# Matmuls of constants on TensorE in three pauses of a two-layer transformer kernel

## The chip, the core and the metric

The kernel runs on one core of one Trainium2 chip. A core has five engines with instruction queues of their own, which are synchronised by semaphores: TensorE (PE in the profile; its loads of stationary operands are listed apart, as PEld) for matmuls and transposes, VectorE (DVE), ScalarE (ACT), GpSimd (POOL), and SyncE (SP), which here only starts DMAs. TensorE reads SBUF and writes PSUM, which has eight banks; DVE and ACT empty them. The metric is the time of one execution on the device in microseconds. Lower is better.

## The reference

One batch of 256 tokens of width 1024 goes through two different layers, all in float32:

```
x = first_block(x, mem, ...)      # mixer (differential attention + gated linear attention),
                                  # cross attention, mixture of experts
return second_block(x, mem_2, ...)  # three attention branches, gated merge, final RMS norm

# the piece of the first block around its experts
xf = rmsnorm(h, norm_g)
p_group  = softmax(xf @ w_group + b_group)         # 4 groups
e_logits = xf @ w_expert + b_expert                # 32 experts, 8 of a group
top_p, top_i = top_k(softmax(e_logits of the group), 2)
hid = silu(xb @ w_gate[e]) * (xb @ w_up[e]);  out = hid @ w_down[e]
```

Each expert has two 1024x512 matrices and one of 512x1024. All 32 are read, 192 MiB in float32.

## The kernel before

The program is written engine by engine: one function per engine holds its instructions in the order in which they run, and semaphores tie the functions together. Nothing schedules them anew. The order on TensorE is thus the order of the calls in its function, and the two names that matter most in it are:

- `turn(names, src)`: transposes a 256x1024 activation in blocks of 128x128, four of them into a PSUM bank, through `transpose` (line 1989), a matmul with the identity `ident`. `turn_normed(prefix, src)` does so after it has waited for `normed_ready`, that is for a row norm. It is called in front of each dense stage: `x` (the start), `mem`, `h1`, `h2` (in front of the router), `h3` (in front of the second layer). ACT and DVE empty the four banks, for most of these stages as a rounded high part (ACT, line 746) and a rounded low part (DVE, line 1191). For `h2` they copy them unrounded (ACT line 707, DVE line 1168).
- `dense(name, x, uses, ...)`: a product with 1 MiB-halves of a weight block in three matmuls (lines 2044 to 2046: high x high, high x low, low x high). Each half has first been split by ACT (line 761) and DVE (line 1205). `moving` and `standing` call it.

**Stages around the change.** At the start, PE transposes the gain rows (`cols`), waits until ACT has squared the input, POOL has made the inverse roots and DVE has scaled the rows (line 1158), transposes `x`, and begins with the low-rank gate product (line 2076) and the dense blocks. In front of the router, the dense blocks `co0` and `co1` end the cross attention. DVE adds them to `h` (line 1494), the row norm follows (line 1568 on DVE), PE transposes it, runs the router product of 16 matmuls with 36 columns (line 2302), then the dense block `xv2`, which belongs to the second layer, and then the five small matmuls that rank tokens within experts (lines 2309 to 2313). Before the second layer, `scatter` (line 2382) adds the last experts' outputs to `h` through DVE (line 1688), PE loads a flag (`over_flag`) that says whether any expert has more than 32 tokens, jumps over the extra rounds if none has, and transposes the norm of `h`.

**The experts** go in eight quads of four experts, each on 32 rows of the array. SP brings their weights in units of 4 MiB (line 588) into buffers of which some are parts of `ring` and `uT`, which the dense stages use before. Its DMAs wait in order: the piece of `uT` is free when the router product has read it, the first slots of `ring` when `xv2` has.

**PSUM.** `PSUM_PLAN` gives the eight banks in turn to a list of names. `wait_free(name)` waits, if the bank had an earlier use, until that has been emptied, and returns the bank. It changes no state.

**Constants.** `ident` and `ones` are float32 tiles of 128x128 that POOL makes at the start. PE's first wait covers both.

Of the kernel before, what the change touches and what calls it, by code (L numbers as in the profile page):

```python
# [31 lines left out]
P = 128  # L32
# [178 lines left out]
def build(nc, A, out):  # L211
    with ExitStack() as ctx:
        def sb(name, shape, dt=F32):
            return ctx.enter_context(nc.sbuf_tensor(name, shape, dt))
# [27 lines left out]
        ident = sb("ident", [P, P])  # L242
        ones = sb("ones", [P, P])
# [48 lines left out]
        bank = [ctx.enter_context(nc.psum_tensor(f"bank{b}", [P, 512], F32)) for b in range(8)]  # L292
# [135 lines left out]
        def wait_free(name):  # L428

            b, k = USE[name]  # L430
            if k:
                nc.tensor.wait_ge(drained[b], k)
            return bank[b]
# [4 lines left out]
        def full(name, ins):  # L438
            ins.then_inc(filled[USE[name][0]], 1)
# [1539 lines left out]
        def _(pe):  # L1979
            mm = nc.tensor.matmul  # L1980
# [6 lines left out]
            def transpose(dst, src):  # L1987
                k = src.shape[0]
                return nc.tensor.transpose(dst, src, ident[0:k, 0:k])  # L1989
# [7 lines left out]
            def turn(names, src):  # L1997

                for c2, name in enumerate(names):
# [4 lines left out]
                                             src[:, t, (2 * c2 + c) * P:(2 * c2 + c + 1) * P])  # L2004
                    full(name, last)

            def turn_normed(prefix, src):
                pe.wait_ge(normed_ready, 2 * ROW_NORMS.index(prefix) + 2)
                turn([f"{prefix}T{c}" for c in range(4)], src)

            def wait_turned(prefix, n=4):
                for c in range(n):
                    wait_drained(pe, f"{prefix}{c}")
# [39 lines left out]
            def moving(name, x, before_half=None):  # L2053

                dense(name, x, [f"{name}_{t}" for t in range(TT)], False, before_half)
# [8 lines left out]

            b = wait_free("cols")
            full("cols", transpose(b[:, 0:N_COLS], rows[0:N_COLS, :]))
            turn_normed("x", normed)
            wait_turned("xT")
            pe.wait_ge(gates_landed, 16 * 2)
            b = wait_free("grT")  # L2070
# [3 lines left out]
            for k in range(KC):  # L2074
                for part, (w, x) in enumerate(((w_hi, x_hi), (w_hi, x_lo), (w_lo, x_hi))):
                    last = mm(b[0:16, 0:T], w[:, k, :], x[:, k, :], start=k + part == 0,
                              stop=k == KC - 1 and part == 2)
# [3 lines left out]
            b = wait_free("z")  # L2081
            for pair in range(2):
                last = mm(b[:, pair * T:(pair + 1) * T], gate_w[:, pair * P:(pair + 1) * P], grT[:, :],
                          start=True, stop=True)
# [64 lines left out]
            for ch in (1, 2, 3):  # L2149
                o = GLA_CHUNK * (ch % 2)  # L2150
                for r in range(2):
                    lo = (2 * (ch // 2) + r) * DV
                    for odd in range(2):
# [3 lines left out]
                                  start=False, stop=True, skip_group_check=True)  # L2157
# [93 lines left out]
            for hp in range(2):  # L2251
                for t in range(TT):
                    b = wait_free(f"cs{t}_{hp}")
                    for n in range(2):
                        for k in range(2):
                            c = 2 * (2 * hp + n) + k
                            last = mm(b[:, n * T:(n + 1) * T], cq3[:, c, t * P:(t + 1) * P], ck3[:, c, :],  # L2257
                                      start=k == 0, stop=k == 1)
# [19 lines left out]
            for hh in range(H1):  # L2278
                if hh + 1 < H1:
                    c_turn(hh + 1)  # L2280
                b = wait_free(f"co_{hh}")
# [9 lines left out]
            moving("co0", parts(coT, lo_a))  # L2291
            moving("co1", parts(coT, lo_a))

            turn_normed("h2", normed)
            wait_turned("h2T")
            pe.wait_ge(params_landed, 16 * N_PARAMS)
            b = wait_free("logits")
            NE = N_EXPERTS
            w = N_GROUPS + NE
            for t in range(TT):  # L2300
                for k in range(KC):
                    last = mm(b[:, t * w:(t + 1) * w], uT[:, k, t * P:(t + 1) * P], w_router[:, k, :],
                              start=k == 0, stop=k == KC - 1)
# [4 lines left out]
            b = wait_free("rank")  # L2308
# [68 lines left out]
            def scatter(S, n):  # L2377

                pe.wait_ge(S.y_ready, n + 2)
                for t in range(TT):  # L2380
                    for half in range(2):
                        mm(bank[(6, 2)[t] + half][:, :], gate_mat[:, t * P:(t + 1) * P],
                           y_slots[:, half * 512:half * 512 + 512], start=True, stop=True)\
                            .then_inc(S.scattered, 1)
# [11 lines left out]
            quad(QUADS // 2 - 1, 0)  # L2396
            experts(moe, QUADS // 2 - 1, 1)
            scatter(moe, QUADS - 1)
            pe.wait_ge(moe.added, 4 * QUADS + 4)
            pe.wait_ge(router_step, 2)  # L2400
            over = pe.value_load(over_flag[0:1, 0:1], min_val=0, max_val=1)
# [12 lines left out]
            b = wait_free("ikw")  # L2414
            for t in range(TT):
                w = HD + H2
                for part, x in enumerate((as_chunks(as_f32(uT_flat)), as_chunks(as_f32(lo_a)))):
                    for k in range(KC):
                        last = mm(b[:, t * w:(t + 1) * w], x[:, k, t * P:(t + 1) * P], w_ikw[:, k, :],
                                  start=part + k == 0, stop=part == 1 and k == KC - 1)  # L2420
# [5 lines left out]
            b = wait_free("ikT")  # L2426
# [195 lines left out]
```

## Time and profile before

| | |
|---|---|
| median of 3 runs | 1115.41 us (1115.09 to 1117.59) |
| the profiled execution | 1117.33 us |
| its span in the profile | 1115.6 us |
| PE busy | 885.5 us, 79% |
| DVE busy | 457.3 us, 41% |
| ACT busy | 318.8 us, 29% |
| TensorE clock granted, mean | 0.901 |
| HBM read | 290.25 MB |

The profile shows one execution, in us from the span's start. Its chain of what ended last consists of PE work, DMA and time in which an engine waited for nothing that is shown. PEclk is the clock that TensorE was granted, in parts of 2.4 GHz: the rows know 1.00 (2.4 GHz) and 0.50 (1.2 GHz), and numbers between are means over both. From about 324 to 784 us the DMA engines are busy throughout with the experts' weights. Before and after that, PE is the busiest engine.

### The profile page before, as it was taken

How to read it: one execution, taken by the hardware profiler on the slowest of the kernel's cores; microseconds unless marked ns; L12 is line 12 of the kernel's file. 1: busy time of each engine (PE TensorE's matmuls, PEld its weight loads, DVE VectorE, ACT ScalarE, POOL GpSimd, SP SyncE). 2: the span in 40 equal slices, each digit the busy share in tenths (PEclk: the TensorE clock that was granted, in tenths of full speed). 3: DMA queues.
4: the chain of work that ended last, by engine and by line, in shares of the span. 5: the costliest groups of instructions: out<-in, count | busy, mean ns of one | idle time of the engine just before them, and what ended most of it. 6: DMA issues, size and time to landing. Idle time of an engine off the chain costs nothing.

```text
span 1115.6 us, 13486 instructions
## 1 busy us (share of the span) xinstructions
PE 885.5 (79%) x5425; PEld 611.7 (55%) x5425; DVE 457.3 (41%) x839; ACT 318.8 (29%) x509; POOL 21.6 (2%) x34
## 2 busy tenths in 40 slices
PE   5999988888787767565757576575699999999996
PEld 4777867677672313121313122131388799999985
DVE  4668773563541202020201102010447768765584
ACT  4646642553300000000000000000323455555432
POOL 1020010000000000000000000000000000000000
PEclk9999998899889888697878878887699999999998
DMA  7553453322959999999999999999335444444440
GB/s 264 186 165 98 167 189 120 108 77 97 374 219 422 421 421 422 421 422 421 422 422 422 421 422 421 421 421 416 116 116 186 155 156 145 150 152 151 141 162 38
DMA packets 75200, 292.05 MB, mean 262 GB/s; under 512 B 9522, under 2 KB 9868, under 8 KB 50572
## 3 DMA queue, kind: packets, MB, share of 16 engines
q1 hardware_dynamic: 72812, 288.48, 66.8%
q10 hardware_dynamic: 2336, 2.84, 0.7%
q8 instruction: 37, 0.61, 0.2%
q14 instruction: 15, 0.12, 0.0%
HBM read 290.25 MB, written 1.05 MB: 261 GB/s over the span
## 4 chain that ended last, share of the span: by engine, by line
issue 30%; PE 27%; DMA 27%; SPq 7%; DVE 6%; ACT 2%; POOL 1%; DVEq 0%; POOLq 0%; ACTq 0%
DMA ring<-in_w_e_down 10%; DMA ring<-in_w_e_gate 9%; SPq L588 7%; DMA ring<-in_w_e_up 7%; PE bank L2044 5%; PE bank L2046 5%; PE bank L2045 5%; PE bank L2351 5%; PE bank L2370 2%; DVE ring_rounded L1205 2%; ACT ring_rounded L761 1%; DVE ring_rounded L1191 1%; PE bank L2257 1%; PE bank L2286 1%; PE bank L1989 1%
## 5 line engine op out<-in xcount | busy, mean ns | idle before, releaser
L1205 DVE TENSOR_TENSOR ring_rounded<-ring,ring_rounded 128x2048 fp32r<-128x2048 f32 x80 | 183.2, 2291 | 170.0 <-ACT ring_rounded L761 169.7
L761 ACT ACTIVATE ring_rounded<-ring 128x2048 fp32r<-128x2048 f32 x80 | 152.9, 1913 | 229.6 <-PE bank L2046 229.6
L2351 PE MATMUL bank<-ring,main 128*32 128x512 f32 x768 | 116.1, 761 | 71.5 <-DMA ring<-in_w_e_up 47.1
L2045 PE MATMUL bank<-ring_rounded 128*128 128x256 f32 (+1 forms) x512 | 159.2, 311 | 0.0
L2046 PE MATMUL bank<-ring_rounded 128*128 128x512 f32 x368 | 146.8, 399 | 0.0
L2351 PEld LDWEIGHTS bank<-ring,main 128*32 128x32 f32 x768 | 28.4, 134 | 156.0 <-issue 74.0
L2370 PE MATMUL bank<-ring,main 128*32 128x512 f32 x384 | 64.7, 834 | 47.2 <-DMA ring<-in_w_e_down 47.2
L2044 PE MATMUL bank<-uT_rounded,ring_rounded 128*128 128x256 f32 x352 | 101.7, 289 | 0.0
L2045 PEld LDWEIGHTS bank<-ring_rounded 128*128 128x128 f32 x512 | 98.2, 192 | 5.0
L2046 PE MATMUL bank<-uT_rounded,ring_rounded 128*128 128x256 f32 x352 | 99.5, 283 | 0.0
L2044 PE MATMUL bank<-ring_rounded,uT_rounded 128*128 128x512 f32 x224 | 90.6, 404 | 8.6 <-DVE ring_rounded L1191 4.3
L2045 PE MATMUL bank<-ring_rounded,uT_rounded 128*128 128x512 f32 x224 | 88.7, 396 | 0.0
L2046 PEld LDWEIGHTS bank<-ring_rounded 128*128 128x128 f32 x368 | 70.9, 193 | 15.7
L1680 DVE COPY main<-bank 128x512 f32<-128x512 f32 x8 | 5.5, 692 | 162.3 <-PE bank L2328 162.3
L2044 PEld LDWEIGHTS bank<-uT_rounded,ring_rounded 128*128 128x128 f32 x352 | 67.4, 191 | 1.7 <-issue 1.4
L2046 PEld LDWEIGHTS bank<-uT_rounded,ring_rounded 128*128 128x128 f32 x352 | 67.4, 191 | 0.0
L2370 PEld LDWEIGHTS bank<-ring,main 128*32 128x32 f32 x384 | 14.6, 148 | 94.8 <-DMA ring<-in_w_e_down 51.9
L1675 DVE SCALAR_TENSOR_TENSOR main<-main,bank 128x512 f32<-128x512 f32 x8 | 5.5, 688 | 144.3 <-PE bank L2351 144.3
L2044 PE MATMUL bank<-ring_rounded 128*128 128x512 f32 x128 | 51.8, 405 | 5.9 <-DVE ring_rounded L1191 3.5
L2044 PEld LDWEIGHTS bank<-ring_rounded,uT_rounded 128*128 128x128 f32 x224 | 43.1, 192 | 20.1 <-issue 7.6
L2351 PE MATMUL bank<-main 128*32 128x512 f32 x192 | 37.4, 737 | 19.2 <-DMA uT<-in_w_e_up 19.2
L984 ACT ACTIVATE main<-bank 128x512 f32<-128x512 f32 x8 | 4.8, 597 | 162.3 <-PE bank L1989 162.3
(274 smaller groups left out, 1260.5 us busy)
## 6 DMA issues: line engine op xcount, KB each, us to landing
ring<-in_w_e_gate SPq DMA_DIRECT2D x48, 1024.0 KB, 26.3
ring<-in_w_e_up SPq DMA_DIRECT2D x48, 1024.0 KB, 26.7
ring<-in_w_e_down SPq DMA_DIRECT2D x48, 1024.0 KB, 26.6
ring<-in_w_in SPq DMA_DIRECT2D x46, 1024.0 KB, 5.0
main<-in_w_e_up SPq DMA_DIRECT2D x12, 1024.0 KB, 26.7
main<-in_w_e_gate SPq DMA_DIRECT2D x12, 1024.0 KB, 26.2
main<-in_w_e_down SPq DMA_DIRECT2D x12, 1024.0 KB, 26.9
ring<-in_w_ckv SPq DMA_DIRECT2D x8, 1024.0 KB, 5.0
```

Source lines behind the costliest of these rows:

```text
L588: sp.dma_start(weight_unit(b, at + i, chunks), w_of[e, :, h * n:(h + 1) * n, :])\
L761: a.activation(rounded(hi_half(h)), raw_half(name, h), ACT.Copy).then_inc(hi_made, 1)
L1191: last = v.scalar_tensor_tensor(rounded(lo[:, at]), src[:, at], gain, as_f32(hi[:, at]), ALU.mult, ALU.subtract)
L1205: v.tensor_tensor(rounded(raw), raw, as_f32(hi_half(h)), ALU.subtract).then_inc(split_made, 1)
L1989: return nc.tensor.transpose(dst, src, ident[0:k, 0:k])
L2044: mm(dst, left[0], right[0], start=first, stop=False, skip_group_check=True)
L2045: mm(dst, left[0], right[1], start=False, stop=False, skip_group_check=True)
L2046: last = mm(dst, left[1], right[0], start=False, stop=last_one, skip_group_check=True)
L2257: last = mm(b[:, n * T:(n + 1) * T], cq3[:, c, t * P:(t + 1) * P], ck3[:, c, :], start=k == 0, stop=k == 1)
L2286: last = mm(b[:, c * T:(c + 1) * T], cv3[:, kt, lo:lo + P], c_pT[hh % 2][:, kt * T:(kt + 1) * T], start=kt == 0, stop=kt == 1)
L2351: last = mm(bank[2 + part][on, :], xg3[:, h * (KC // 2) + k, on], weight_unit(unit_buffer(p, u), e, KC)[:, k, :], start=h + k == 0, stop=h ...
L2370: last = mm(bank[4 + half][on, :], hidT3[:, c, on], weight_unit(unit_buffer(p, u), e, FC)[:, k, half * 512:half * 512 + 512], start=c == 0 ...
```

## The change

A helper issues matmuls of `ident` with `ones` into a PSUM bank that something else overwrites later, with no signal and nothing that reads the result. It is called at three places: with 12 matmuls between the transpose of `cols` and the transposes of `x`, with 18 between `co1` and the transposes of `h2`, and with 20 between the last scatter and the load of `over_flag`.

```diff
+            def keep_busy(b, n):
+
+                for _ in range(n):
+                    mm(b[:, 0:P], ident[:, :], ones[:, :], start=True, stop=True)
+
             def turn_normed(prefix, src):
                 pe.wait_ge(normed_ready, 2 * ROW_NORMS.index(prefix) + 2)
                 turn([f"{prefix}T{c}" for c in range(4)], src)
...
             full("cols", transpose(b[:, 0:N_COLS], rows[0:N_COLS, :]))
+            keep_busy(wait_free("xT0"), 12)
             turn_normed("x", normed)
...
             moving("co1", parts(coT, lo_a))

+            keep_busy(wait_free("h2T0"), 18)
             turn_normed("h2", normed)
...
             scatter(moe, QUADS - 1)
+            keep_busy(bank[0], 20)
             pe.wait_ge(moe.added, 4 * QUADS + 4)
             pe.wait_ge(router_step, 2)
             over = pe.value_load(over_flag[0:1, 0:1], min_val=0, max_val=1)
```

On TensorE at the start of the program, before (`rows` are the gains, `normed` the normed input):

```order
L1989 MATMUL bank<-ident,rows 128x74 [waits rows_landed,consts_made]
L1989 MATMUL bank<-ident,normed 128x128 [waits normed_ready]
L1989 MATMUL bank<-ident,normed 128x128 x15
L2076 MATMUL bank<-uT_rounded,main_rounded 16x256 [waits bank_drained4,gates_landed,bank_drained3,low_rank_weights_split,bank_drained2,bank_drained1]
L2076 MATMUL bank<-ring_rounded,main_rounded 16x256
```

and after:

```order
L1989 MATMUL bank<-ident,rows 128x74 [waits rows_landed,consts_made]
L2010 MATMUL bank<-ones,ident 128x128 x12
L1989 MATMUL bank<-ident,normed 128x128 [waits normed_ready]
L1989 MATMUL bank<-ident,normed 128x128 x15
L2082 MATMUL bank<-uT_rounded,main_rounded 16x256 [waits bank_drained4,gates_landed,bank_drained3,low_rank_weights_split,bank_drained2,bank_drained1]
```

The 12 matmuls stand ahead of the instruction that waits for `normed_ready`, and wait for nothing themselves. Nothing else has moved. Lines behind the helper are 5 to 8 higher than before.

On TensorE in front of the router, after (`w_router` x `uT` is the router product). Before, the two rows of line 2010 are missing and the rest is the same:

```order
L2051 MATMUL bank<-ring_rounded 128x512
L2010 MATMUL bank<-ones,ident 128x128 [waits bank_drained2]
L2010 MATMUL bank<-ones,ident 128x128 x17
L1989 MATMUL bank<-ident,normed 128x128 [waits bank_drained2,normed_ready]
L1989 MATMUL bank<-ident,normed 128x128 x3
```

The bank that the first of them waits for was emptied before `co0` began. The norm is waited for behind the last.

On TensorE before the second layer, after (`main` x `main` is the last scatter, the load reads the flag):

```order
L2389 MATMUL bank<-main 128x512 x3
L2010 MATMUL bank<-ones,ident 128x128 x20
L2409 TENSOR_LOAD over_flag [waits router_step,moe_added]
L2409 ISA x2
L2410 COMPARE_AND_BRANCH
```

The 20 matmuls stand between the scatter and the load of the flag, so that load, the branch and the transposes of `h3` queue up behind them.

## Rows read from the trace of the kernel before

**Rows 1.** Timeline of PE: start us, us, instructions [idle before <-releaser].
```profile
11.50 3.67 PE L1989 MATMUL bank<-ident,normed 128*128 128x128 f32 x16 [5.08 <-DVE normed L1158]
...
298.96 3.67 PE L1989 MATMUL bank<-ident,normed 128*128 128x128 f32 x16 [6.92 <-DVE normed L1568]
...
797.18 3.67 PE L1989 MATMUL bank<-ident,normed 128*128 128x128 f32 x16 [6.52 <-DVE normed L1158]
```
**Rows 2.** Timeline of PE at the start, behind the transposes.
```profile
17.32 0.37 PE L2076 MATMUL bank<-uT_rounded,main_rounded 128*16 128x256 f32 x1 [2.15 <-DVE ring_rounded L1191]
...
19.63 0.63 PE L2076 MATMUL bank<-uT_rounded,main_rounded 128*16 128x256 f32 x2
...
20.61 0.40 PE L2076 MATMUL bank<-uT_rounded,main_rounded 128*16 128x256 f32 x2
```
**Rows 3.** Timeline of DVE at the start: the emptying of the transposes.
```profile
13.66 3.30 DVE L1191 SCALAR_TENSOR_TENSOR ring_rounded<-bank,cols,uT_rounded 128x256 fp32r<-128x256 f32 x8 [1.44 <-ACT uT_rounded L746]
```
**Rows 4.** The instructions of one line: a plain float32 matmul, called once.
```profile
L2313 PE MATMUL bank<-assigned,ones x2: 276/276/276, 324.0 to 324.1; 128*128 128x32 f32 x2
```
**Rows 5.** Stretches, PE, within the gather: from:to length, busy (x), PEclk, DMA share, GB/s.
```profile
327.45:330.80 3.35, 3.18 (x15) 0.50 1.01 426
330.86:332.90 2.04, 2.04 (x20) 1.00 1.01 414
```
**Rows 6.** Stretches, PE, around pauses in front of other stages.
```profile
197.74:201.12 3.38, 3.38 (x16) 0.50 0.00 0
201.16:204.54 3.38, 1.27 (x6) 1.00 0.00 0
204.57:207.95 3.38, 3.38 (x10) 0.50 0.02 5
231.80:235.25 3.45, 0.94 (x6) 1.00 0.00 0
235.29:238.67 3.38, 3.38 (x10) 0.50 0.02 5
267.80:273.00 5.20, 3.42 (x15) 1.00 0.00 0
```
**Rows 7.** Stretches, PE, from `co1` through the router product into `xv2`.
```profile
292.10:296.70 4.60, 0.00 (x0) 1.00 1.01 417
296.72:303.70 6.98, 3.67 (x16) 0.50 1.02 423
303.73:310.50 6.77, 6.77 (x32) 0.50 0.80 332
310.55:313.77 3.22, 3.22 (x9) 0.50 0.55 173
```
**Rows 8.** Timeline of DVE in front of the router.
```profile
298.74 2.28 DVE L1205 TENSOR_TENSOR ring_rounded<-ring,ring_rounded 128x2048 fp32r<-128x2048 f32 x1
300.97 0.69 DVE L1168 COPY uT<-bank 128x512 f32<-128x512 f32 x1
```
**Rows 9.** Stretches of `xv2` and of the experts: PE, PEld, DVE, ACT, POOL, PEclk, DMA, GB/s.
```profile
314.50:323.90 9.40, 9.40 (x47) 7.79 (x45) 2.65 (x10) 0.30 (x2) 0.00 (x0) 1.00 0.05 19
324.00:784.00 460.00, 300.30 (x1888) 105.61 (x1891) 60.53 (x194) 25.66 (x46) 0.00 (x0) 0.83 1.01 420
```
**Rows 10.** Stretches, PE, before the second layer.
```profile
790.70:795.05 4.35, 0.00 (x0) 1.00 0.02 6
795.07:803.00 7.93, 3.67 (x16) 0.50 0.01 2
803.01:808.70 5.69, 5.69 (x14) 0.50 0.00 0
```
**Rows 11.** Timeline of DVE before the second layer.
```profile
792.24 0.15 DVE L1221 COPY marks<-ones 128x1 f32<-128x1 f32 x1 [0.85 <-issue]
...
797.04 2.28 DVE L1205 TENSOR_TENSOR ring_rounded<-ring,ring_rounded 128x2048 fp32r<-128x2048 f32 x1
799.25 3.40 DVE L1191 SCALAR_TENSOR_TENSOR ring_rounded<-bank,cols,uT_rounded 128x256 fp32r<-128x256 f32 x8
```

## The prediction

> **What bounds the kernel now.** I read PE's waits for a norm first, in the timeline. It is idle for 5.08 us at the start, 6.92 us in front of the router and 6.52 us before the second layer [rows 1]. PE can't work in any of the three, since the norm goes through ACT, POOL and DVE one after the other. The change doesn't shorten these waits. What it can change is the clock behind them, so I read the granted clock next, by stretches. In front of the router it is 1.00 in the pause until 296.70 and 0.50 from then through the transposes, all of the router product and 3.2 us of `xv2` [rows 7]. Before the second layer it is 0.50 from 795.07 to 808.70, of which 5.69 us are matmuls [rows 10]. At the start the durations tell it: a pair of 256-column matmuls takes 0.63 us at 19.63 and 0.40 us at 20.61 [rows 2], so the full clock comes at about 20.2 us.
>
> Then I asked what each stretch is worth. Up to `xv2` the kernel is a chain of PE, DVE and ACT, so time saved on PE mostly stays saved. The end of `xv2` frees the ring: the DMA engines are nearly idle (0.05) in its last 9.4 us and full (1.01) in the 460 us of expert weights after it [rows 9]. That long stage runs at the speed of the DMA, so a shift of the end of `xv2` shifts everything behind it by as much. The faster clock within the experts would be worth nothing, and the change doesn't touch it.
>
> **What is added.** A plain float32 matmul leaves two records [rows 4], so the calls are 24, 36 and 40 instructions. I take their price from the gather, whose matmuls have the same type and 128 columns: 3.18 us for 15 is 0.212 us at half clock, 2.04 us for 19 to 20 is 0.105 us at full clock [rows 5].
>
> - Start: from about 6.4 to 11.5 us PE is free, 5.1 us [rows 1]. At half clock 24 x 0.212 = 5.1 us, so at worst they end 0.1 us late; if the clock rises on the way they end by about 10.8.
> - Router: the clock is full when `co1` ends at 292.05, so 36 x 0.107 = 3.9 us, to 295.9. The norm comes at 298.96 [rows 1]: 3.0 us of pause are left.
> - Second layer: the clock is full at 790.70 [rows 10], so 40 x 0.107 = 4.3 us, to 795.0. The load of the flag and the branch, queued behind, have the 2.2 us until 797.18 [rows 1]. No row shows them on PE. DVE needs 0.85 us for the same flag and branch [rows 11], so the norm covers them; at half clock it would not (third rival).
>
> **Does the clock survive what is left of the pauses?** Rows 6 is the test. At 201.16 the clock had just come back. PE paused for 2.1 us, then the matmuls ran for 1.27 us at the full clock and fell to half for 3.4 us. In the 3.45 us from 231.80 PE was idle for 2.5 us, and it is the same story: the matmuls had the full clock for 0.8 us and then half for 3.4 us. Only the pause of 1.8 us in front of `co0` left it at 1.00. After the change the pauses are 3.0 us in front of the router's transposes, then 2.15 us or more behind the 16 transposes at the start (2.15 in [rows 2], and up to 1.8 us longer where the transposes get faster but the work behind them doesn't), and likewise before the second layer. All are longer than those that lost the clock. So I expect that the added matmuls keep the clock up in the pause in which nothing happens anyway, and that it falls a little later, in part of the useful work.
>
> The trace says more on transposes: 16 of them and nothing else from 197.74 to 201.12 at half clock, and behind them the full clock [rows 6]. The Trainium skill says of this, in "TensorE: Matmul & The Clock Gate", section "Part 4: PE-mode transpose", that in transpose mode the full clock does not engage, as it isn't counted as busy in the same way. By that rule the transposes would be more pause, the clock would be lost at all three places before the useful matmuls, and the sum below would shrink to 0.4 us. The measurement decides, and it says that transposes count.
>
> **The sum.**
>
> 1. Start. At half clock the transposes go in steps of 0.212 us too (16 in 3.38 us [rows 6]). DVE's part of the emptying starts after ACT has the first bank, and then takes 3.30/8 = 0.41 us a piece [rows 3], which is as fast as PE delivers now. So only the first four transposes count: 4 x (0.212 - 0.107) = 0.42 us earlier. From 17.32 to 20.2, 2.9 us, matmuls run at half clock, which costs about 1.3 us. With the change the pause in front of them grows to 3.7 us, so the clock should fall in or shortly behind it, and stay down for about 3.4 us as in rows 6, part of which lies in the pause. Gain between 0 and 0.42 + 1.3 = 1.7; I take 0.7.
> 2. Router. The copies of the transposes are held by DVE's split until 300.97 [rows 8]; from there two copies of 0.69 follow each other, and the router could start at 302.7 instead of 303.73: at most 1.0 us. The product is 32 instructions at 0.212 = 6.8 us; at full clock 32 x 0.107 = 3.4 us: at most 3.4 us. `xv2` has 3.2 us at half clock, which cost half of it or a little less, 1.5 us. All of it would be 5.9 us. But the matmuls end at 295.9, and from pauses of 2.1 to 4.6 us the clock fell 3.4 to 4.7 us behind the last instruction (292.05 to 296.70, 790.66 to 795.05, 201.1 to 204.55 [rows 6, 7, 10]). That is 299.3 to 300.6 here, in the transposes. They can bring it back, as at 201.12, but the router product can't keep it: at half clock its 6.8 us did not raise it [rows 7]. So some of the transposes and of the router run fast, and `xv2` begins slow again for about as long. It can also lose: where the clock falls at the end of the router, `xv2` has it at half for longer than the 3.2 us of now, up to 1.2 us of loss. Between -1.2 and 5.9; I take 1.0, a share of the transposes and a fraction of the router.
> 3. Second layer. DVE splits weights until 799.3 and begins the emptying only then [rows 11], so faster transposes bring nothing at all, and the matmuls still start at 803.0. The transposes then end at 799.0, and the pause to 803.0 is 4.0 us, longer than any that kept the clock. It falls, and comes back about 3.4 us or more later, against 5.69 now. Between 0 and 2.65 us (14 matmuls in 5.69 us against 0.228 each, the step in `co0` in rows 6); I take 0.2.
>
> Together 0.7 + 1.0 + 0.2 = 1.9 us. From the profiled execution's 1117.33 us this gives 1115.4. That execution is 1.9 us above the median of the runs, 1115.41, so against the runs it is 1113.5 us, 0.17% faster. What a measurement of this kernel can tell from no change is about 0.2%, 2.2 us: the runs alone spread over 2.5 us.
>
> **The rivals.**
>
> - *The clock holds at all three places.* Then the gain is 1.7 + 5.9 + 2.65 = 10.3 us, 1105.1 us. For it: the clock is full when two of the three begin. Against it: rows 6, and the router product itself. 0.08.
> - *Nothing useful is reached.* The clock falls in the rest of each pause before the real work, the transposes at the start give 0.4 us, and the time is 1115.0. For it: two of three pauses that remain are longer than 2.5 us, and before the second layer only DVE decides the start. 0.28.
> - *Slower: the added matmuls run at half clock and overrun.* In front of the router 36 x 0.212 = 7.6 us against 6.9 of pause, 0.7 us late; before the second layer 40 x 0.212 = 8.5 us, to 799.2, and with 0.85 us for flag and branch 800.1 against 797.18, 2.9 us late, which DVE's emptying passes on. With the loss of 1.2 us in `xv2` this is 4.8 us, less 0.4 at the start, 4.4: 1119.8 us. It decides where the clock is low when `co1` or the scatter ends. Against it: both rows show 1.00 there [rows 7, 10]. A milder form, only the later fall in `xv2`, gives 1116.2. 0.12 together.
>
> The forecast, a clock that falls later and in part of the work, has 0.52, and its own range is 1111.5 to 1115.4.
>
> **How the numbers follow.** Faster by over 0.2% are the first rival, about half of the forecast (0.27) and a little of the second: 0.37. Slower by over 0.2% is half of the third and some noise: 0.10. Within is 0.53. The range leaves out most of the first and the worst of the third: 1109.0 to 1117.0.
>
> **What would show it.** In the profile after, the granted clock by stretches: 1.00 until about 299 us in front of the router; then, if I am right, 0.50 again within the router product or at the start of `xv2`. The router product at 6.8 us would show its step wrong; at 3.5 us and `xv2` full from its start, the first rival. The matmuls of the second layer should start 12.3 us behind the last scatter as now and have 3 to 6 us at 0.50. The three added groups should take about 4.4, 3.9 and 4.3 us; 7.6 or 8.5 would be the third rival. A gain that isn't at these places would make the argument wrong even if the time fits.

## The result, and the profile after

The changed kernel takes 1118.05 us (median of 10 runs, 1115.35 to 1119.84) against 1115.15 us for the kernel before (10 runs, 1113.53 to 1117.59). The ratio is 1.0023, with a 95% interval of 1.0012 to 1.0034: slower by about 2.6 us, with 1 outside the interval. Its ten runs fall into two groups, six at 1117.97 to 1119.84 us and four at 1115.35 to 1116.01, where the kernel before lies too; the one that was profiled is of the first group, so what the other four did isn't seen. Of the executions further down, a single one, of the kernel with only the start changed, took 2119.92 us and is left out of its ratio as a slow one. The profiled executions are closer, 1118.12 us after and 1117.33 us before, because the one of before lies 2.2 us above its median. So the question for the profile is not where 0.8 us went but which stages moved.

Up to the experts the added matmuls ran as the forecast said. The timeline of PE after (start us, us, instructions, idle before and its releaser), which answers to [rows 1, 2]:

```profile
6.05 5.14 PE L2010 MATMUL bank<-ones,ident 128*128 128x128 f32 x24
11.29 1.97 PE L1989 MATMUL bank<-ident,normed 128*128 128x128 f32 x16
16.59 0.28 PE L2082 MATMUL bank<-uT_rounded,main_rounded 128*16 128x256 f32 x1 [3.33 <-DVE ring_rounded L1191]
...
17.17 0.40 PE L2082 MATMUL bank<-uT_rounded,main_rounded 128*16 128x256 f32 x2
...
18.11 0.63 PE L2082 MATMUL bank<-uT_rounded,main_rounded 128*16 128x256 f32 x2
...
290.22 4.18 PE L2010 MATMUL bank<-ones,ident 128*128 128x128 f32 x36
297.30 3.55 PE L1989 MATMUL bank<-ident,normed 128*128 128x128 f32 x16 [2.90 <-DVE normed L1568]
301.94 4.86 PE L2309 MATMUL bank<-w_router,uT 128*128 128x36 f32 x32 [1.09 <-DVE uT L1168]
```

At the start the 16 transposes take 1.97 us instead of 3.67, but the gate product follows 5.30 us behind their start instead of 5.82: DVE's emptying sets the rest. The pairs of 256-column matmuls begin at 0.40 us each and are at 0.63 again from 18.11. In front of the router the product takes 4.86 us instead of 7.02. The same stretches by clock, PE after (from:to, length, busy, PEclk, DMA share, GB/s), beside [rows 7]:

```profile
290.20:294.40 4.20, 4.20 (x37) 1.00 1.00 417
294.45:297.45 3.00, 0.15 (x1) 1.00 1.00 412
297.50:300.85 3.35, 3.35 (x16) 0.50 1.01 421
300.90:301.90 1.00, 0.00 (x0) 1.00 1.04 434
301.94:304.25 2.31, 2.31 (x21) 1.00 1.00 413
304.35:306.80 2.45, 2.45 (x13) 0.50 1.01 415
307.00:311.00 4.00, 4.00 (x10) 0.50 0.84 287
311.20:319.80 8.60, 8.60 (x39) 1.00 0.01 3
```

The clock holds through the pause of 3.0 us, is at half for the transposes, comes back for the first 21 of the router's 32 records and is at half again until 311, well into `xv2`. From the end of `co1` to the end of `xv2` it is 29.42 us (290.38 to 319.80) against 31.08 before (292.05 to 323.13).

Not all of that belongs to the change. Two runs of the experiments below show the router product the other way round. This is its row in a kernel without the 18 matmuls (the third group alone):

```profile
302.77 4.98 PE L2307 MATMUL bank<-w_router,uT 128*128 128x36 f32 x32 [1.09 <-DVE uT L1168]
```

and in one with them (the first two groups alone):

```profile
301.25 7.01 PE L2309 MATMUL bank<-w_router,uT 128*128 128x36 f32 x32 [1.09 <-DVE uT L1168]
```

Over the eleven profiles with the 18 matmuls there or none, it takes 4.86, 4.89, 7.01 and 7.01 us in the four kernels with the 18 matmuls, and 4.95 to 5.00 in four kernels without any in this place and 7.01 to 7.02 in the other three. So the course of the granted clock differs between executions of the same instructions. What the 18 do shift in every profile is where it falls first: 7.1 to 8.3 us behind the end of `co1` with them, 3.7 to 4.8 us without.

Of the 3.3 us by which `xv2` ended earlier, the last scatter kept 2.4: it ended at 788.3 instead of 790.7.

Before the second layer more than that was lost again. PE after, beside the third line of [rows 1]:

```profile
784.58 3.70 PE L2389 MATMUL bank<-main 128*128 128x512 f32 x8 [0.72 <-ACT main L992]
788.12 4.63 PE L2010 MATMUL bank<-ones,ident 128*128 128x128 f32 x40
795.45 0.41 PE L1989 MATMUL bank<-ident,normed 128*128 128x128 f32 x2 [2.70 <-DVE normed L1158]
798.41 3.25 PE L1989 MATMUL bank<-ident,normed 128*128 128x128 f32 x14 [2.55 <-issue]
803.80 0.76 PE L2049 MATMUL bank<-ring_rounded,uT_rounded 128*128 128x512 f32 x1 [2.15 <-DVE ring_rounded L1191]
```

Two transposes run at the full clock, and then nothing for 2.55 us, put down to "issue": PE waited for nothing that the profile's semaphores show. Before, all 16 stood in one row [rows 1]. The first dense matmul starts 15.5 us behind the scatter's end instead of 12.3 (790.67 to 803.01): 3.2 us.

The first two transposes are late as well, though their row names the norm. The norm on DVE, and the branch on PE's sequencer, in after (the second line is the view of a source line: duration in ns three times, start in us):

```profile
793.33 1.41 DVE L1158 TENSOR_SCALAR normed<-h,rstd 128x1024 f32<-128x1024 f32 x2 [0.81 <-POOL rstd L662]
```

```profile
L2410 PEldq COMPARE_BRANCH  x1: 3704/3704/3704, 791.6 to 791.6; - x1
```

The norm was ready at 794.74. The branch took 3.70 us, until 795.3, and the first transpose started at 795.45, 0.7 us behind the norm; before it was 0.05 us (797.13 to 797.18).

What PE waited for between the second transpose and the third stands in a view that one doesn't look at for an idle engine: the DMA queues. Queue 8 is of the kind "instruction". From the stretch of after from 794 to 797 us (the digits and the GB/s are 40 equal slices):

```profile
DMA  0000000000000000000000000070000000000000
GB/s 0 0 0 0 0 0 0 0 0 0 0 0 0 0 0 0 0 0 0 0 0 0 0 0 0 0 218 0 0 0 0 0 0 0 0 0 0 0 0 0
...
q8 instruction: 1, 0.02, 1.8%
```

One packet, in the 27th slice, at 795.97 us; another one lies at 792.63. In the kernel before they are at 793.35 and 796.70. Over the whole span the page of after has this line for the queue (packets, MB, share):

```profile
q8 instruction: 39, 0.64, 0.2%
```

That is 16.4 KB a packet. The reading that fits, and that the experiments test: PE takes its instructions in such pieces, and this branch, which is taken, finds none of those behind it there. One piece is fetched 1.0 us into the branch, the next 3.3 us later. In after, the first piece ended behind the second transpose, and the third ran 2.44 us behind the second fetch.

The granted clock there was low, as forecast. PE after, by stretches, beside [rows 10]:

```profile
792.80:795.80 3.00, 0.35 (x2) 1.00 0.00 0
795.84:803.78 7.94, 3.26 (x15) 0.50 0.01 2
803.80:809.40 5.60, 5.60 (x13) 0.50 0.01 3
```

### The profile page after: what moved, and what is told of

Its sections match the earlier page's. It is cut to its first block, busy times and chain, and to the rows that moved or that the text cites. A ratio compares the mean times of both kernels' runs of the same rounds, so it can differ in the third digit from the quotient of the medians.

```text
span 1116.4 us, 13686 instructions
## 1 busy us (share of the span) xinstructions
PE 888.1 (80%) x5525; PEld 619.7 (56%) x5525; DVE 457.5 (41%) x839; ACT 318.4 (29%) x509; POOL 21.6 (2%) x34
## 4 chain that ended last, share of the span: by engine, by line
issue 30%; PE 27%; DMA 26%; SPq 8%; DVE 6%; ACT 2%; POOL 1%; DVEq 0%; POOLq 0%; ACTq 0%
DMA ring<-in_w_e_down 11%; SPq L588 8%; DMA ring<-in_w_e_up 7%; DMA ring<-in_w_e_gate 7%; PE bank L2049 5%; PE bank L2051 5%; PE bank L2050 5%; PE bank L2358 4%; PE bank L2377 3%; DVE ring_rounded L1205 2%; ACT ring_rounded L761 1%; DVE ring_rounded L1191 1%; PE bank L2335 1%; PE bank L2292 1%; PE bank L2263 1%
## 5 line engine op out<-in xcount | busy, mean ns | idle before, releaser
L2358 PE MATMUL bank<-ring,main 128*32 128x512 f32 x768 | 113.9, 748 | 78.1 <-DMA ring<-in_w_e_up 54.6
L2377 PE MATMUL bank<-ring,main 128*32 128x512 f32 x384 | 62.0, 805 | 51.4 <-DMA ring<-in_w_e_down 51.4
L984 ACT ACTIVATE main<-bank 128x512 f32<-128x512 f32 x8 | 4.8, 597 | 161.5 <-PE bank L1989 161.5
L992 ACT ACTIVATE main<-bank 128x512 f32<-128x512 f32 x16 | 9.6, 597 | 138.7 <-PE bank L2377 138.7
```

Source lines behind the costliest of these rows:

```text
L2358: last = mm(bank[2 + part][on, :], xg3[:, h * (KC // 2) + k, on], weight_unit(unit_buffer(p, u), e, KC)[:, k, :], start=h + k == 0, stop=h ...
L2377: last = mm(bank[4 + half][on, :], hidT3[:, c, on], weight_unit(unit_buffer(p, u), e, FC)[:, k, half * 512:half * 512 + 512], start=c == 0 ...
```

## The experiments

Two theories about the 3.2 us stood against each other. Either the branch simply comes too late (20 matmuls are ahead of it), or the added instructions have moved the place at which PE goes on within a 16 KB piece. A plain float32 matmul has a weight load and a matmul twice, so 50 of them are 200 more PE instructions (13686 against 13486 in all). "Stage" below is the time from the end of the last scatter to the first dense matmul of the second layer, read from each run's profile; the ratio is that of the timed runs, with its interval.

**The first two groups alone.**

Edits of this kernel and the next two stand against the changed one.

```diff
             scatter(moe, QUADS - 1)
-            keep_busy(bank[0], 20)
```

> The changed kernel without the third group (the 20 matmuls between the last scatter and the load of the flag). Theory A: the changed kernel loses its time in front of the second layer alone, where TensorE stands still for 2.6 us after two transposes of h3, because instructions behind the branch are not there yet. Without the third group the branch comes right after the last addition again, so the stretch from the end of the last scatter to the first dense matmul is 12.3 us as before (15.5 in the changed kernel), and what the second group saves in front of the router stays: 1.5 to 2.5 us faster than before, ratio 0.998. Theory B (rival): the loss is spread, by the clock or by the DMA of the expert stage that ran dry for about 1 us. Then this kernel is at 1.000 to 1.002 of before.

Ratio 0.9995 [0.9986, 1.0004]; the stage is back at 12.34 us. So the loss needs the third group, and the two others bring next to nothing: the 0.998 that I expected was too much. 0.9995 and 3.2 us (0.0028) make 1.0023, the result.

**The third group alone.**

```diff
-            keep_busy(wait_free("xT0"), 12)
             turn_normed("x", normed)
             ...
-            keep_busy(wait_free("h2T0"), 18)
             turn_normed("h2", normed)
```

> The kernel before with only the third group of 20 matmuls. Theory A1, the late branch: the 20 matmuls delay the load of the flag and the branch by 1.7 us or more, and with them the fetch of the instructions behind it. Then 15 us or more from the end of the last scatter to the first dense matmul (12.3 before) and 2 to 3 us slower than before. Theory A2, the place of the branch's target in the 16 KB blocks in which instructions are fetched (the 100 added instruction pairs of all three groups have moved it): here it is moved by 80 instructions and not by 200, so the border lies elsewhere, about 120 instructions behind the target; then 12.3 us and no change in time.

Ratio 1.0001 [0.9990, 1.0012], stage 12.27 us. The same 20 matmuls ahead of the branch, and no stall between transposes. The first of them is 0.7 us behind the norm as in the changed kernel (794.91 to 795.59), but DVE is still splitting weights until 797.1 and begins to empty the banks then, so that costs nothing. A late branch by itself, as late as here, isn't enough.

**All three groups, with the place behind the branch moved on.** 14 more matmuls in the body that the branch skips make 256 added instructions, one whole piece.

```diff
             with pe.If(over):
                 ...
                 pe.wait_ge(moe.added, 4 * (1 + MORE_ROUNDS) * QUADS + 4)
+                keep_busy(bank[0], 14)
```

> The changed kernel with 14 more of the same matmuls inside the branch that is never taken. They run not at all, but with the 50 added ones they are 64 x 4 = 256 instructions of 64 bytes, one whole 16 KB block, so the target of the branch lies in its block where it lay before. Theory A2 (place in the block): no stall of 2.6 us after two transposes, 12.3 us from the scatter's end to the first dense matmul, 1.5 to 2.5 us faster than before. Theory A1 (late branch): a stall as in the changed kernel, 15 us, and 2 to 3 us slower than before.

PE of this run: the 16 transposes stand in one row again, behind the same 40 records.

```profile
789.91 4.63 PE L2010 MATMUL bank<-ones,ident 128*128 128x128 f32 x40
797.07 2.67 PE L1989 MATMUL bank<-ident,normed 128*128 128x128 f32 x16 [2.53 <-DVE normed L1158]
```

Stage 12.25 us, ratio 0.9997 [0.9986, 1.0007]. The fetch behind the branch is as late as in the changed kernel (4.3 us behind the scatter's end in both), only the place in the piece differs, and the 14 matmuls more are never executed. The expected gain in the time, 1.5 to 2.5 us against before, didn't come, for the same reason as in the first experiment.

**The place alone, without one executed matmul more.** The kernel before, with 50 matmuls in the skipped body.

```diff
                 pe.wait_ge(moe.added, 4 * (1 + MORE_ROUNDS) * QUADS + 4)
+                keep_busy(bank[0], 50)
```

> The kernel before with 50 of the matmuls inside the branch that is never taken, and none anywhere else: nothing more is executed, the branch is as early as before, and its target lies in its block as in the changed kernel. Theory A2: a stall after two transposes, but a shorter one, since the fetches start 1.7 us earlier against the norm: the second block was fetched 3.35 us behind the first in both kernels and work went on 2.4 us behind that, so at 799.1 instead of 797.5; 14 us from the scatter's end to the first dense matmul and 1.5 to 2 us slower than before. Theory A1: 12.3 us and no change.

```profile
794.44 0.69 PE L1989 MATMUL bank<-ident,normed 128*128 128x128 f32 x2 [6.53 <-DVE normed L1158]
796.34 3.15 PE L1989 MATMUL bank<-ident,normed 128*128 128x128 f32 x14 [1.22 <-issue]
```

Two, a stall, fourteen: the same break at the same transpose. Stage 13.71 us, 1.4 over before; the ratio, 1.0007 [0.9995, 1.0019], can't tell 1.4 us from nothing, but the rows can. (In this execution the dense matmuls behind it also had the full clock for part of the time, 302.73 us from the first of them to PE's last against 303.81 before, which hides most of it.)

**Late alone, and late with the place moved.** PE waits for ACT's squares of `h` (the first part of the h3 norm) ahead of the flag, so that the branch comes 3.2 us later behind the scatter than before (these two hold only for inputs that don't take the extra rounds); the second has the 50 in the skipped body as well.

```diff
             scatter(moe, QUADS - 1)
+            in_order(pe, row_squared, ROW_NORMS, "h3")
             pe.wait_ge(moe.added, 4 * QUADS + 4)
```

> The kernel before, none of the matmuls added; TensorE only waits for ACT's squares of h3 before it waits for the last addition and loads the flag, so that the branch comes about 3 us later, at 794.6 instead of 791.6 (its norm comes at 797.2). It is fit for inputs alone that don't take the branch. Theory A1 (a late branch is enough for the loss): 15 us from the scatter's end to the first dense matmul, 2.5 us slower. Theory A2 (place in the block is needed): the branch's first block is fetched at 796 and is there before or just at the norm, 12.3 to 13 us, 0 to 0.7 us slower.

```profile
799.94 3.65 PE L1989 MATMUL bank<-ident,normed 128*128 128x128 f32 x16 [8.89 <-issue]
```

> The late branch of the run before and 50 matmuls inside the branch that is never taken, none executed: both suspected parts of the changed kernel without its matmuls. Fit for inputs alone that don't take the branch. If place and lateness make up the loss together, the second block is fetched 3.3 us behind the first and work goes on 1.5 to 2.4 us later: 15.5 us or up to 1.5 us more (the branch is even later than in the changed kernel), 3 us or more slower than before. If the matmuls themselves have a part in it, 14 us at most.

```profile
798.74 0.66 PE L1989 MATMUL bank<-ident,normed 128*128 128x128 f32 x2 [8.38 <-issue]
801.54 3.15 PE L1989 MATMUL bank<-ident,normed 128*128 128x128 f32 x14 [2.14 <-issue]
```

Late alone: stage 14.76 us, ratio 1.0017 [1.0006, 1.0028]. I had expected 12.3 to 13, so this was a miss: beyond some point lateness costs by itself. The row gives the point. The fetch was at 797.43 and the first transpose at 799.94, 2.5 us later, when the norm had been there for 2.4 us (since 797.51). Both together: 16.46 us, 1.0027 [1.0016, 1.0038].

Six profiles fall into one sum. The first dense matmul starts 5.3 us behind the third transpose (5.34 before, 5.39 after, 5.29 with the place alone, 5.30 in the last kernel; 5.43 with late alone, and 5.0 in the kernel with the place moved on, whose transposes began at the full clock). The third transpose runs with the first two, unless the piece ends between them, and then it comes 2.2 to 2.7 us behind the second fetch. All times from the scatter's end:

| kernel | first fetch | second fetch | first transpose | third | stage |
|---|---|---|---|---|---|
| before | 2.68 | 6.03 | 6.51 | 7.00 | 12.34 |
| all three groups | 4.34 | 7.68 | 7.16 | 10.12 | 15.51 |
| same, place moved on | 4.30 | 7.61 | 6.99 | with the first | 12.25 |
| place alone | 2.65 | 5.72 | 6.52 | 8.42 | 13.71 |
| late alone | 6.38 | 9.45 | 8.89 | with the first | 14.76 |
| late and place | 5.88 | 8.95 | 8.37 | 11.17 | 16.46 |

So the changed kernel needed both halves: the fetch 1.7 us later, and the piece that ends at the wrong place. The place alone would have cost 1.4 us, a lateness of 1.7 us alone nothing.

**What do covered pauses give?** The forecast said that the clock falls because 2 to 3 us of pause remain. The next three runs fill them. The router's alone first: 27 matmuls ahead of the norm, and 8 behind the transposes, in the copies' pause.

```diff
+            keep_busy(wait_free("h2T0"), 27)
             turn_normed("h2", normed)
+            keep_busy(wait_free("logits"), 8)
             wait_turned("h2T")
```

> The matmuls in front of the router alone, but without a pause left: 27 of them before the transposes of h2 and 8 between these and the router product. Theory C: the 18 of the change bring nothing because the 3 us left bring the clock down later; here it is at 1.00 through transposes and into the router product, but the router product lets it fall in its course and xv2 starts at half. From the end of co1 to the end of xv2 28 to 29.5 us (31.1 before, 29.4 in the changed kernel, 29.5 in two kernels that have nothing there), 0 to 1.5 us faster than before. Rival D: the clock holds through the router product as well: 25.5 us, 5 us faster.

PE of this run, by stretches:

```profile
300.62:304.20 3.58, 3.58 (x32) 1.00 1.01 421
304.24:308.10 3.86, 3.86 (x35) 1.00 1.02 419
308.25:311.50 3.25, 3.25 (x10) 0.50 1.01 407
311.65:320.40 8.75, 8.75 (x40) 1.00 0.18 75
```

Ratio 0.9971 [0.9955, 0.9988], from 12 runs that spread more widely than others, 1105.39 to 1115.52 us. `co1` to `xv2` takes 26.85 us against 29.5 to 31.2 in the kernels with nothing there, with one period of half clock left, at the start of `xv2`.

**All pauses covered**: 12 and 15 around the x transposes, 27 and 8 around those of `h2`, 6 ahead of the flag, 10 behind the branch and 15 in DVE's pause before the second layer:

```diff
             scatter(moe, QUADS - 1)
+            keep_busy(bank[0], 6)
             ...
+            keep_busy(bank[0], 10)
             turn_normed("h3", normed)
+            keep_busy(wait_free("iq_0"), 15)
```

> The best version that the results point to: pauses covered at all three places, before and behind the transposes (12 + 15 at the start, 27 + 8 in front of the router, 6 ahead of the flag, 10 behind the branch and 15 behind the transposes of h3), with only 6 of them ahead of the branch. If a covered pause keeps the clock, 1.7 us at the start, 1 to 5 in front of the router and 2.6 before the second layer are gained: 4 to 8 us faster than before. If the clock falls in spite of it, or the additions are in the way, no change.

```profile
790.64 4.64 PE L2010 MATMUL bank<-ones,ident 128*128 128x128 f32 x20 [3.75 <-issue]
795.07 2.60 PE L1989 MATMUL bank<-ident,normed 128*128 128x128 f32 x16
```

Ratio 0.9957 [0.9940, 0.9974], and the third place spoils part of it. The branch leaves such a hole in every run, 3.75 us here (the branch itself takes 3.3 to 3.9 us in all 14 profiles), which nothing ahead of the branch can fill; the 10 matmuls behind it ran at half clock, 4.6 us instead of 2.1, and held up the transposes: they start at 795.07, and the norm was there at 792.02. Stage 15.22 us.

**The same without the 6 and the 10**, and 8 instead of 15 behind the transposes:

```diff
-            keep_busy(bank[0], 6)
-            keep_busy(bank[0], 10)
-            keep_busy(wait_free("iq_0"), 15)
+            keep_busy(wait_free("iq_0"), 8)
```

> The version with all pauses covered, without the 6 matmuls ahead of the flag and the 10 behind the branch, and 8 instead of 15 behind the transposes of h3: so 12 + 15 at the start, 27 + 8 in front of the router, 8 behind the transposes of h3. The branch comes as early as in the kernel before. If the late transposes of h3 were what held the version with everything covered back, the scatter's end to the first dense matmul is 12.3 to 12.8 us again (15.2 there) and the kernel is 6 to 8 us faster than before. If the gain was limited by something else, 4 us as there.

PE of this run around the second layer and, by stretches, through router and `xv2`:

```profile
789.77 3.67 PE L1989 MATMUL bank<-ident,normed 128*128 128x128 f32 x16 [6.52 <-DVE normed L1158]
793.24 2.18 PE L2010 MATMUL bank<-ones,ident 128*128 128x128 f32 x16
```

```profile
297.49:301.10 3.61, 3.61 (x32) 1.00 1.03 424
301.11:304.90 3.79, 3.79 (x35) 1.00 1.00 411
305.00:315.80 10.80, 10.80 (x48) 1.00 0.48 198
...
793.75:795.55 1.80, 1.67 (x15) 1.00 0.00 0
```

1107.45 us against 1115.41, ratio 0.9931 [0.9919, 0.9944]: faster than both kernels. Stage 12.34 us, and from the first dense matmul of the second layer to PE's last it is 301.12 us instead of 303.81. It has 62 added matmuls ahead of the branch's target, 248 instructions, more than the 200 of the changed kernel, and no break in the transposes; 248 is 8 short of the 256 that put the place back where it lay before, which fits, but was not measured apart.

**The three places of it alone.** The router with the changed kernel's 18 and nothing behind the transposes; the start with 12 and 15; the second layer with 8 behind the transposes:

```diff
+            keep_busy(wait_free("h2T0"), 18)      # one kernel: this alone
+            keep_busy(wait_free("xT0"), 12)       # another: these two alone
             turn_normed("x", normed)
+            keep_busy(wait_free("grT"), 15)
             ...
             turn_normed("h3", normed)
+            keep_busy(wait_free("iq_0"), 8)       # a third: this alone
```

> The 18 matmuls in front of the router alone, as in the change. Theory C: with 3 us of pause left the clock still falls, before or in the router product, and the end of co1 to the end of xv2 stays within what kernels without them show (29.5 to 31.1 us); time within 0.1% of before. The forecast's step said 1.0 us faster, 0.999.

Ratio 1.0010 [1.0000, 1.0020]. Its router product and `xv2`, PE by stretches:

```profile
302.75:306.05 3.30, 2.29 (x21) 1.00 1.02 422
306.20:312.80 6.60, 6.60 (x22) 0.50 0.88 333
```

The half clock lies differently than in the profile of before, less of it in the router's matmuls and more in `xv2`: until 312.8, from a product that ended at 308.65, so 4.2 us of `xv2` instead of 3.2 [rows 7]. But a kernel without these 18, the third group alone, has the same picture (4.98 us for the product, `xv2` at half until 311.8), and 29.56 us from `co1` to the end of `xv2` against 29.48 here.

> Only the start: 12 matmuls before the transposes of x and 15 behind them. The version with everything covered had the full clock here from 11.4 us on without a break. 0.4 us for the first four transposes and 1.3 us for the gate product, 1.7 us faster than before, ratio 0.9985. Rival: ACT's and DVE's splits of the weights behind hide the faster gate product, then 0.4 us or nothing.

Ratio 0.9986 [0.9977, 0.9995]. Its gate product starts 5.29 us behind the first transpose (5.30, 5.39 and 5.65 in the three profiles with 12 alone, 5.76 to 5.86 in those without), and has the full clock throughout. The interval stays below 1.

> Only 8 matmuls behind the transposes of h3, where DVE's emptying leaves a pause of 2 us. The transposes run at half clock from 797.2 and the clock comes back 3 to 6 us later if work goes on without a pause, so at 800 to 803, in front of the dense blocks instead of 5.7 us into them: 1 to 2.6 us faster than before, with the first dense matmul 12.3 to 13 us behind the scatter's end. Rival: the 8 matmuls run at half clock and are as late as they save, no change.

```profile
792.40:799.05 6.65, 4.39 (x21) 0.50 0.01 2
799.15:800.45 1.30, 1.30 (x13) 1.00 0.00 0
800.48:806.20 5.72, 5.72 (x26) 1.00 0.00 0
```

Ratio 0.9978 [0.9970, 0.9987] for 8 matmuls. 26 dense matmuls in 5.7 us at the full clock stand against 14 in 5.69 at half [rows 10], 2.7 us less to PE's end (301.10 us from the first dense matmul to PE's last, 303.81 before). One profile alone would not show that this is the edit's: the kernel with only the router's pauses covered has 301.10 too, with nothing added here. But all three kernels with matmuls behind these transposes have 301.10 to 301.21, and of the eleven without them only that one; the others have 302.64 to 303.99. And the timed runs show the gain. The ratios of the three places alone, 0.9986, 0.9971 and 0.9978, multiply to 0.9935; the kernel with all three has 0.9931.

## Why the prediction was wrong, step by step

**The step that failed** is the one on the second layer in "What is added": "The load of the flag and the branch, queued behind, have the 2.2 us until 797.18 [...] so the norm covers them." The queue behind the 20 matmuls was named, but the price of a taken branch was read from DVE's 0.85 us. "No row shows them on PE" is wrong: the trace of before has the branch, in the view of its source line.

```profile
L2402 PEldq COMPARE_BRANCH  x1: 3643/3643/3643, 792.3 to 792.3; - x1
```

It took 3.64 us on PE, 3.70 in after, and 0.07 us on DVE (line 1705). So the norm did not cover load and branch: the first transpose came 0.7 us behind it. That part cost nothing, since DVE was still splitting weights (the third group alone has the same 0.7 us and a stage of 12.27). The part that cost was a term the sum didn't have, the second piece of instructions: 792.63 + 3.34 + 2.44 is 798.41, the third transpose's start. It came 10.12 us behind the scatter's end instead of 7.00, and the stage became 3.2 us longer, where the sum had 0. The rival on the slower side had the right place and nearly the right size for it, 2.9 us, but by another mechanism, matmuls at half clock; they ran at the full clock, 4.63 us for 40 records.

The trace of before also has the two fetches: in the DMA view of the pause behind the scatter there is one packet of instructions at 793.35 and one at 796.70. And the count of added instructions gave the shift. What it could not give is where in its piece the branch's target lies. The Trainium skill has the size that joins them, in "Perfetto Trace Analysis", section "The 4-stage abstract model": an instruction is 64 bytes. By that a packet of 16.4 KB is 256 instructions, and the kernel with 256 added ones, whose stage is 12.25 us, agrees.

**The durations of what is added** were right: 5.14, 4.18 and 4.63 us against 4.4, 3.9 and 4.3. The one at the start came nearer to its stated worst case of 5.1, and still ended in time.

**The start: 0.7 us was forecast.** The first four transposes give 0.52 (5.82 to 5.30) against 0.42, so DVE's share was placed right. In the profile of after the clock fell between 17.17 and 18.11, in the gate product, as the step says; in the runs with the first two groups alone and with the place moved on it stayed full all through. The kernels without any edit there are no steadier: `co1` ends at 290.27 in the one with only the 8 matmuls far behind it and at 292.05 in before. One profile can't size this term. The timed runs can: together with the router 0.9995, 0.6 us with an interval from -0.4 to 1.6, where I had 1.7.

**The router: 1.0 us was forecast,** between -1.2 and 5.9. The profile of after shows the forecast's course: full clock through the pause, transposes at half, part of the router at full, `xv2` at half for longer (about 4.5 us, until 311.1, instead of 3.2). That is luck in part, since only the first of these is the change's doing in every profile: two of the four kernels with the 18 have the whole product at half (7.01 us), and four of the seven without them have part of it at full (4.95 to 5.00). That the transposes count as activity was right too: at 301.94, behind 16 of them at half clock, it was 1.00, again against the rule of the Trainium skill in "TensorE: Matmul & The Clock Gate", section "Part 4: PE-mode transpose", that in transpose mode the full clock doesn't engage. These 18 alone measure 1.0010, 1.1 us slower with an interval from 0 to 2.2. The way from `co1` to the end of `xv2` takes 29.4 to 30.6 us in the four kernels with them and 29.5 to 31.2 us in the seven with nothing there, so that the executions differ by more than the edit could be seen to give. The term put a share of the gain on a course of the clock that comes with and without the change; its zero and below were as likely as 1.0. Why the timed runs are rather slower than faster with the 18 alone stays open.

**The second layer: 0.2 us was forecast** for the clock, and the clock did fall and stay down as said (0.50 from 795.84 to 809.40). The start of the matmuls "12.3 us behind the last scatter as now" failed, by the step above; with the place moved on it is 12.25, so without the break it would have held. The bound of 2.65 us is 2.50 by the step's own numbers (5.69 less 14 x 0.228); where the clock was full from the start of these matmuls, 2.7 us were measured.

**The experts** pass a shift on, but not whole here: `xv2` ended 3.3 us earlier and the scatter 2.4. In the first 23 us of the expert weights the DMA moved less per second than before. All engines, first after, then before (PE, PEld, DVE, ACT, POOL, PEclk, DMA, GB/s):

```profile
318.66:341.66 23.00, 18.89 (x154) 10.98 (x156) 9.71 (x48) 1.47 (x3) 0.00 (x0) 0.93 0.88 351
```

```profile
322.00:345.00 23.00, 18.90 (x154) 10.91 (x156) 9.70 (x48) 1.47 (x3) 0.00 (x0) 0.93 0.91 368
```

17 GB/s over 23 us is 0.39 MB, 0.9 us at the 420 GB/s of [rows 9]. That is the 0.9 us that is missing; why the DMA was slower there stays open, and two single profiles don't show that it is so in every run.

## What to carry to other kernels

Work put ahead of a branch on an engine that is "idle anyway" delays the fetch of everything behind it, and any change in the number of instructions, skipped ones included, moves where the first fetched piece ends: before moving or adding instructions around a branch, read the DMA view for packets of the instruction queue in the pause behind it, read the branch's own row (3.3 to 3.9 us here), and see how many instructions lie between the target and the end of its piece. Compare more than two profiles before a course of the clock is put down to an edit: the same instructions met it at different levels here. Matmuls that are to keep the clock up brought something in the timed runs here only where no long pause was left between them and the work (0.9931 with the pauses covered, 0.9995 for two groups with 3 us left behind each), and put behind the last dependency of the pause, right ahead of the work, eight of them gave more (0.9978) than all fifty of the changed kernel did even without the stall (0.9997).

## What the runs showed of the hardware that was not expected

- The taken branch in front of the second layer took 3.3 to 3.9 us on PE in all 14 profiles. Where nothing else held it up, PE's first matmul behind it started 2.5 to 2.8 us after the fetch of the first 16 KB piece (797.43 to 799.94, 796.25 to 798.74, 792.63 to 795.45). The second piece was fetched 3.0 to 3.6 us after the first, and where the first had run out, work went on 2.2 to 2.7 us behind that. In the three profiles with a stall, which the profile calls "issue", PE had come to the end of its first piece behind the second transpose, 0.4 to 0.7 us after it had started; the third came 1.9 to 3.0 us after that start.
- Matmuls in a body that is never executed changed the time of the stage: 50 of them 12.34 to 13.71 us, 14 of them 15.51 to 12.25.
- The router product (36 columns a matmul) had the full clock in all three kernels with its pauses covered. `xv2` behind it had it throughout in one (1.00 until 315.80), and in the two others the clock fell at 308.2 and 304.96, within 1 us of the start of `xv2`, for 3.4 us. One of these has the same instructions up to there as the first, so it is the execution that tells them apart; what sets the moment stays open.
